# Layer 0's eight later modulation pieces in two bf16 passes, their low halves made by GpSimd, and the pieces spread over the whole input projection

## The reference, cut to what matters

```python
for layer in range(DEPTH):
    m_l = jnp.split(silu_c @ ada_w[layer] + ada_b[layer], 6, axis=-1)      # ada_w[layer]: 1024 x 6144
    m_c = jnp.split(silu_cc @ ada_w[layer] + ada_b[layer], 6, axis=-1)
    h_l = rmsnorm(x, norm_mix_g[layer]) * (1 + m_l[1]) + m_l[0]
    h_c = rmsnorm(ctx, norm_mix_g[layer]) * (1 + m_c[1]) + m_c[0]
    p_l, p_c = h_l @ w_in[layer], h_c @ w_in[layer]                        # w_in[layer]: 1024 x 3840
    ...
    x = x + m_l[2] * (mixed @ w_out[layer])
    h2 = rmsnorm(x, norm_ffn_g[layer]) * (1 + m_l[4]) + m_l[3]
    x = x + m_l[5] * channel_mixer(h2)
```

## Time and profile before

| | us |
|---|---|
| median of 3 runs | 1772.24 (1771.97 to 1772.33) |
| profiled execution, its own time | 1774.29 |
| its span, first to last instruction | 1772.4 |
| TensorE busy | 1704.0 (96%) |
| TensorE weight loads busy | 1084.0 (61%) |
| VectorE busy | 1224.6 (69%) |
| ScalarE busy | 377.2 (21%) |
| GpSimd busy | 236.2 (13%) |
| mean granted TensorE clock | 0.997 of 2.4 GHz |

### The profile page before, as it was taken

How to read it: one execution, slowest core, us unless ns; L and a number is a source line. 1 busy time by engine, 2 the same in 40 slices (tenths; PEclk the granted TensorE clock), 3 DMA queues, 4 the chain that set the end, 5 groups by cost and what they waited for, 6 DMA issues and landing times.

```text
span 1772.4 us, 34791 instructions
## 1 busy us (share of the span) xinstructions
PE 1704.0 (96%) x15369; PEld 1084.0 (61%) x15369; DVE 1224.6 (69%) x1286; ACT 377.2 (21%) x695; POOL 236.2 (13%) x108
## 2 busy tenths in 40 slices
PE   6999999899999999999999888999999999999999
PEld 2334557674544444445465555968787787869695
DVE  1443476975444344115576877999999999999998
ACT  1101254453422222112125342010100000001100
POOL 0035100020656430000460010000000000000000
PEclk9999999999999999999999999999999999999999
DMA  9932201014656425231230126999999999999994
GB/s 375 329 143 72 95 1 48 1 49 152 229 193 235 181 104 190 71 95 48 96 119 1 48 106 259 407 410 419 412 419 413 418 407 419 414 415 414 411 416 189
DMA packets 98846, 408.77 MB, mean 231 GB/s; under 512 B 14009, under 2 KB 20857, under 8 KB 84369
## 3 DMA queue, kind: packets, MB, share of 16 engines
q1 hardware_dynamic: 96504, 405.54, 58.3%
q10 hardware_dynamic: 2200, 1.08, 0.2%
HBM read 405.55 MB, written 1.05 MB: 229 GB/s over the span
## 4 chain that ended last, share of the span: by engine, by line
PE 76%; DVE 8%; PEld 5%; issue 4%; DMA 3%; ACT 2%; PEldq 0%; ACTq 0%; SPq 0%; POOL 0%; DVEq 0%; POOLq 0%
PE PS L1669 12%; PE PS L803 10%; PE PS L2044 9%; PE PS L1627 6%; PE PS L2018 5%; PE PS L2020 5%; PE PS L2021 5%; PE PS L807 5%; PE PS L1533 2%; PE PS L485 2%; DMA ARENA<-in_moe_w 2%; PE PS L1395 2%; DVE ARENA L2140 2%; PEld PS L2044 2%; DVE ARENA L1008 1%
## 5 line engine op out<-in xcount | busy, mean ns | idle before, releaser
L2140 DVE TENSOR_TENSOR ARENA<-ARENA 128x2816 bf16<-128x2816 f32 (+2 forms) x184 | 567.0, 3121 | 23.7 <-DMA ARENA<-in_moe_w 22.6
L2018 PE MATMUL PS<-ARENA 128*128 128x96 bf16 x2816 | 379.1, 209 | 4.9 <-issue 1.9
L2020 PE MATMUL PS<-ARENA 128*128 128x96 bf16 x2816 | 378.9, 209 | 1.7 <-issue 1.5
L2021 PE MATMUL PS<-ARENA 128*128 128x96 bf16 x2816 | 378.8, 206 | 1.3 <-issue 1.0
L2020 PEld LDWEIGHTS PS<-ARENA 128*128 128x128 bf16 x2816 | 354.8, 126 | 9.6 <-issue 9.5
L2018 PEld LDWEIGHTS PS<-ARENA 128*128 128x128 bf16 x2816 | 346.3, 123 | 11.6 <-issue 9.5
L2021 PEld LDWEIGHTS PS<-ARENA 128*128 128x128 bf16 x2816 | 298.6, 106 | 2.1 <-issue 2.1
L803 PE MATMUL PS<-ARENA 128*128 128x512 bf16 (+1 forms) x1104 | 227.9, 356 | 0.0
L2044 PE MATMUL PS<-ARENA 128*96 128x512 bf16 x960 | 216.1, 384 | 0.2 <-DVE ARENA L2140 0.2
L1669 PE MATMUL PS<-ARENA 128*128 128x512 bf16 x984 | 215.8, 379 | 0.0
L2044 PEld LDWEIGHTS PS<-ARENA 128*96 128x96 bf16 x960 | 116.2, 122 | 93.1 <-issue 0.3
(11 more groups left out here) (252 smaller groups left out, 1820.2 us busy)
## 6 DMA issues: line engine op xcount, KB each, us to landing
ARENA<-in_moe_w SPq DMA_DIRECT2D x128, 1408.0 KB, 13.3
ARENA<-in_moe_w SPq DMA_DIRECT2D x48, 1536.0 KB, 16.0
ARENA<-in_ada_w SPq DMA_DIRECT2D x24, 2048.0 KB, 10.2
ARENA<-in_ffn_w SPq DMA_DIRECT2D x15, 2048.0 KB, 7.9
ARENA<-in_w_in SPq DMA_DIRECT2D x11, 2048.0 KB, 8.1
ARENA<-in_moe_w SPq DMA_DIRECT2D x16, 1024.0 KB, 15.8
ARENA<-in_w_in SPq DMA_DIRECT2D x6, 1024.0 KB, 8.7
ARENA<-in_w_out SPq DMA_DIRECT2D x8, 512.0 KB, 4.3
```

The costliest lines, as they stand in the source:

```text
L2018: pe.matmul(out, hi[:, h][:, f], HEH[:, k, :], start=k == 0 and b % 4 == 0, stop=False, skip_group_check=True)
L2020: pe.matmul(out, hi[:, h][:, f], HEL[:, k, :], start=False, stop=False, skip_group_check=True)
L2021: mm = pe.matmul(out, lo[:, h][:, f], HEH[:, k, :], start=False, stop=k == KC - 1, skip_group_check=True)
L2140: dve.tensor_tensor(WLO[q % NSLOT][:, 0:n], RAW[q % NSLOT][:, 0:n], WHI[q % NSLOT][:, 0:n], ALU.subtract).then_inc(S("m_lo"), 1)
```

## The change

Layer 0's pieces 4 to 11 are treated like layer 1's: `pool_ada_halve` makes their low halves, and `pe_ada_mm` multiplies them in two bf16 passes with `SCP`. GpSimd halves pieces 4 to 9 right behind its second norm operation, piece 10 behind the inverse roots of q and k, and piece 11 between the rotations of the two latent tiles. The pieces and the two spreads get other places on TensorE, and the load of piece 11 goes to another place in SBUF (E2) and further back in SP's list.

```diff
                 if L == 0:
-                    for j in {0: (4,), 1: (5, 6, 7), 2: (8, 9), 3: (10, 11)}.get(g, ()):
-                        ada_item(0, j, ("E2", "E1")[j % 2])
+                    for j in {0: (4,), 1: (5, 6, 7), 2: (8, 9), 3: (10,), 4: (11,)}.get(g, ()):
+                        ada_item(0, j, "E1" if j in (5, 7, 9) else "E2")
...
-            if L == 0:
+            if L == 0 and j < 4:
                 parts_of, c = [ada_view(raw_full(pe, ("ada", L, j)))], SC
             else:
                 pe.wait_ge(S("filled"), 5)
-                pe.wait_ge(S("pool_halved"), KC // 2 + 2 * j + 2)
+                pe.wait_ge(S("pool_halved"), 16 + KC // 2 + 2 * j + 2 if L else 2 * (j - 4) + 2)
...
         for j in range(4, 12):
-            ADA_IN_PROJ.setdefault(((2, 3, 4, 5, 8, 9, 10, 11)[j - 4], 0), []).append(("mm", j))
-        for i, first in ((1, 6), (2, 16)):
+            ADA_IN_PROJ.setdefault(((2, 0), (3, 0), (5, 0), (6, 0), (9, 0), (10, 0), (16, 0), (19, 6))[j - 4], []).append(("mm", j))
+        for i, places in ((1, ((7, 0), (7, 2), (7, 4), (7, 6), (8, 1))), (2, ((20, 4), (21, 1), (21, 6), (22, 3), (23, 0)))):
             for step in range(5):
-                ADA_IN_PROJ.setdefault((first + (step > 1), (0, 4, 0, 3, 6)[step]), []).append(("spread", i, step))
+                ADA_IN_PROJ.setdefault(places[step], []).append(("spread", i, step))
...
             for n in range(2 * NT, 5 * NT):
-                if L == 0 and n == 3 * NT:
-                    act_ada_row(act, 0, 2)
                 act_proj_one(act, L, n)
+            if L == 0:
+                act_ada_row(act, 0, 2)
...
-                if L == 0 and n == 6:
-                    for step in range(3):
-                        dve_ada_cp(dve, 0, 1, step)
                 if L == 0 and n == 7:
-                    for step in range(3, 5):
+                    for step in range(4):
                         dve_ada_cp(dve, 0, 1, step)
                 dve_proj_one(dve, L, n)
+                if L == 0 and n == 7:
+                    dve_ada_cp(dve, 0, 1, 4)
...
-            if L == 0:
-                for step in range(5):
-                    dve_ada_cp(dve, 0, 2, step)
-                dve_ada_gain(dve, 0, 4)
             dve_proj_halve(dve, L, "av")
             if L > 0:
                 dve_gates(dve, L, 1)
             for n in range(5 * NT, 6 * NT):
+                if L == 0:
+                    for step in ((0,), (1, 2), (3,), (4,))[n - 5 * NT]:
+                        dve_ada_cp(dve, 0, 2, step)
                 dve_proj_one(dve, L, n)
+            if L == 0:
+                dve_ada_gain(dve, 0, 4)
...
             pool.tensor_tensor(STAT[:, 2, 64:88], STAT[:, 1, 64:88], NEGH[:, 0:24], ALU.pow).then_inc(S(n + "rstd"), 1)
+            if L == 0:
+                pool_ada_halve(pool, 0, 10)
             pool.wait_ge(S(n + "gained"), since(L, n + "gained") + 4)
             for x in LAT_TILES:
+                if L == 0 and x == LAT_TILES[1]:
+                    pool_ada_halve(pool, 0, 11)
...
                 pool_norm_half(pool, 2 * L, 1)
+                if L == 0:
+                    for j in range(4, 10):
+                        pool_ada_halve(pool, 0, j)
                 pool_qk(pool, L)
```

More of the change, by code:

```diff
@@ L452, in ada_halves, with pool_ada_halve @@
             return v[:, :, :, 1], v[:, :, :, 0]
-        def pool_ada_halve(pool, j):
-            raw = raw_full(pool, ("ada", 1, j))
+        def pool_ada_halve(pool, L, j):
+            raw = raw_full(pool, ("ada", L, j))
             hi, lo = ada_halves(raw)
@@ L774, in pe_proj_ready @@
                 if k % 2 == 0:
-                    pe.wait_ge(S("pool_halved"), (KC // 2 + 24) * L + k // 2 + 1)
+                    pe.wait_ge(S("pool_halved"), 16 + (KC // 2 + 24) * L + k // 2 + 1)
                 return
@@ L2370, in _ @@
                     for j in range(12):
-                        pool_ada_halve(pool, j)
+                        pool_ada_halve(pool, 1, j)
                 else:
```

## The result

| | before | changed |
|---|---|---|
| median of 8 runs each, us | 1772.38 (1771.97 to 1774.48) | 1779.24 (1776.74 to 1783.72) |
| ratio of the times | 1 | 1.0037, 95% interval 1.0025 to 1.0048 |
| profiled execution, us (span) | 1774.29 (1772.4) | 1776.84 (1775.0) |
| start of the transposes behind unit 23, us | 199.59 | 204.08 |

The changed kernel is slower by 0.37%, which is 6.6 us; the two medians are 6.9 us apart. The forecast was +2.8 us and 1775.0, its range ended at 1778.5. Its profiled execution was one of its two quickest, only 2.6 us over that of before, so it is best read for places and not for the total.

What follows compares the result with a forecast made beforehand. TensorE, busy 96% of the span, was taken to bound the kernel. Terms -0.9 up to T7, 0 to unit 16, +1.6 low clock and +2.1 behind it gave +2.8 on 1772.24: 1775.0 us, range over cases 1769.0 to 1778.5.

Steps and rivals of the forecast that it cites:

- The two signs: Prediction wrong if unit 16 starts less than 50 us after T7, or piece 5 before 65 or after 67 us.
- T7: The end of projection unit 7 on TensorE, at 109.67 us before the change, where piece 8 started.
- Step 1: Pieces 4 and 5: scalings go first, and piece 5, halved by GpSimd after landing, starts at 65.8, not 60.16; +5.6 us.
- rival (a): At 45.2 us GpSimd's halving gets in before the scalings and alternates with VectorE: +5.3 us; 0.28 together with unheld single-input operations.
- The floor at 65.8: Piece 5 lands at 58.25; 7.2 us of halving plus one or two VectorE instructions in between give 65.8.
- if single-input VectorE operations are not held: TensorE reaches unit 3 by 62 or so, stands 3 to 4 us, gets low clock: total +4.4; 0.28 together with rival (a).
- Steps 2 to 5: Pieces 5 to 7 -2.5; first spread -4.1; T7 to unit 16 0, low clock +1.6; pieces 10 and 11 +2.1 us.
- (b): At unit 16 piece 10's halving runs beside VectorE's nine operations without delaying them, no TensorE wait: -3.1 us, 1769.1; chance 0.10.
- (c): All pieces come in time: -6.6 us for pieces, -3.0 for the wait and clock at 92.68, 1762.6 us; chance 0.02.

Runs made afterwards that it cites:

- scalings first: The change with one wait more: GpSimd starts piece 4 only when VectorE has scaled the latent tokens; 1777.23 us, ratio to before 1.0019.
- 10 and 11 in f32: The change with pieces 10 and 11 left in float32 and not halved, places kept; 1774.63 us, ratio to before 1.0004.
- 4 and 5 in f32: The change with pieces 4 and 5 left in float32 and not halved, places kept; 1771.88 us, ratio to before 0.9982.
- moves alone: The change with no layer 0 piece halved, only the new places and spreads; 1771.86 us, ratio to before 0.9983.
- only 6 to 9 halved: The change with pieces 4, 5, 10 and 11 in float32; 1769.28 us, ratio to before 0.9983; once more 1767.37 us, ratio 0.9967.
- before, first group: The unchanged kernel, run beside the first group of experiments on the same chip; median 1774.26 us.
- before, second group: The unchanged kernel, run beside the second group of experiments on the same chip; median 1774.95 us.
- the change again: The changed kernel measured again without an edit; 1779.63 us, ratio to before 1.0037.
- the kernel with filler matmuls: The change plus useless matmuls, 32 before the turning of the latent tokens and 14 before unit 16; 1798.84 us, ratio to before 1.0130.

## Why the prediction was wrong

**Where each kernel is at the end of the projection.** The stages behind should only shift, so the landmark is the cleanest measure of the sum:

| kernel | transposes start | against before |
|---|---|---|
| before | 199.59 | |
| the change, two profiles | 204.08, 205.39 | +4.5, +5.8 |
| scalings first | 201.75 | +2.2 |
| 10 and 11 in f32 | 202.71 | +3.1 |
| 4 and 5 in f32 | 197.42 | -2.2 |
| moves alone | 196.35 | -3.2 |
| only 6 to 9 halved, two profiles | 192.94, 193.22 | -6.65, -6.4 |

The two signs that it named for being wrong come out one each way: piece 5 came after 67 us (68.72), unit 16 not less than 50 us after T7 (50.66).

**Step 1 failed** ("+5.6 us, a floor: the landing does not depend on anything that the change moves"). The chosen order, scalings first, did not happen; what happened was rival (a), at 0.28, in its first form: GpSimd in first, two operations alternating, 8.09 us where I had worked out 8.6. In each of the four profiles of kernels that halve piece 4 without the extra wait, GpSimd's halving starts 0.06 or 0.07 us ahead of the scaling, so this was no coin toss. Both start on the same power operation's end, at 44.9 to 45.3; the halving stands on the power's own engine, the scaling waits for a signal from another one. The row I had taken against the rival, VectorE's start 0.03 us behind that end, fits this: what stands on the same engine needed no such 0.03 us. The floor at 65.8 was worked out rightly (piece 5 was ready at 65.89) but it wasn't what bound: TensorE came at 68.7, and even in "scalings first" it came to piece 5 without a wait, late by its own low clock. "Scalings first" shows the price of the choice, 2.3 us against the change's first profile.

That the scalings are held at all rested on a case I had left open ("if single-input VectorE operations are not held"). They are: the Trainium skill (SBUF — State Buffer, Who interferes with whom) says that whoever issues first gets the shared pair for the whole instruction, and counts the two-port forms of single-input operations in; the trace agrees, with 8.09 for 1.42 us.

**The low clock was mis-sized, twice.** The prediction gave each wait the 3.2 us at half clock of the earlier trace rows, 1.6 us lost. Behind the 8.13 us wait it was 6.0 us, 3.0 lost. Behind the waits of about 3.5 us at unit 16 it was 3.1 us in one profile and 5.8 in the other, 1.5 and 2.9 lost, and in "scalings first" it was 6.8 us behind the wait of 3.60 us before piece 4. Rival (a) with 3.0 in place of 1.6 would be +6.7 and not +5.3. That this is near the +6.6 of the runs confirms nothing: the landmark of the first profile has +4.5, since TensorE's turning came 6.4 us late and not 7.2, and the steps behind it gave 1.2 us more than they were counted for.

**Steps 2 to 5 held**, but for the low clock at unit 16 in the second profile. From piece 5 to T7 it was 42.55 us where before it was 49.51: -6.96, predicted -2.5 - 4.1 = -6.6. From T7 to unit 16 it was 50.66 us (predicted 51.4), with a wait of 3.44 (predicted 4.3). VectorE's nine operations took 15.1 us (predicted about 15.5). From unit 16 to the transposes, 42.15 us for 38.53 before: +3.6, predicted 1.6 + 2.1. Piece 11 was in time, so were 7 and 9. "10 and 11 in f32" confirms that piece 10's halving alone makes the wait at unit 16. Rivals (b) and (c) did not happen.

**From +4.5 at the landmark to +6.6 in the runs.** Each run lists its span and its mean granted clock; span x (1 - clock) is the time that low clock stands for in it. The clock is listed to 0.001, which is 1.8 us, so a single run says little and a mean more. Of the 8 runs before beside the change only times are on record, so its row has to be compared with the other groups. The means:

| kernel (runs) | span | of it by low clock | the rest |
|---|---|---|---|
| before, first group (32) | 1772.4 | 4.1 | 1768.3 |
| before, second group (23) | 1773.0 | 4.4 | 1768.6 |
| the change (8) | 1777.8 | 9.6 | 1768.2 |
| the change again (11 of 12) | 1778.0 | 10.2 | 1767.8 |
| scalings first (12) | 1775.8 | 8.4 | 1767.4 |
| 10 and 11 in f32 (12) | 1773.5 | 7.1 | 1766.4 |
| 4 and 5 in f32 (12) | 1770.1 | 5.0 | 1765.1 |
| moves alone (11) | 1770.0 | 2.9 | 1767.1 |
| only 6 to 9, two groups (8 of 9, and 5) | 1767.0, 1766.3 | 3.5, 2.8 | 1763.5, 1763.5 |

(Left out are the single runs of 1800.42 and 1790.33, with clocks of 0.981 and 0.983.) The rest is the same before and after the change, within 0.8 us, and what is left over, 5.5 to 5.8 us, is the low clock's column. About 2.0 us of it lie in the wait from 49.0 to 53.1 (4.1 us at 0.50) and are in truth the wait's. So the shorter pieces and the spreads' places paid for all but some 2 us of the waiting, and the low clock cost TensorE some 3.5 us more than before. The prediction's own sum had nothing for this in all, 1.6 off at the first spread and 1.6 on at unit 16, and rival (a) had 1.6. The profiled execution of the change, at 1775.0 x 0.004 = 7.1, has 2.5 us less of it than the mean of its runs, which is why its span understates the change: the kernel before lost 1.7 us in its own profile to a low-clock stretch near 1080 us that the change's first profile lacks. In the second profile the excess lies in longer stretches at the places of the change and in stretches near 24, 925 and 1086 us. The kernel before has such a one at 24 us and one at 1078 us too, behind the same wait of 2.08 us, so these are not the change's doing as such; whether it makes them likelier was not tested and stays open.

## What to carry to other kernels

Work given to an idle helper engine is not free while it shares something with the engine that feeds the bound one: before it is queued, look whom it can get ahead of, and where the feeder has a short operation that the bound engine waits for, put that first by an explicit wait (2.3 us here). Of the two engines that waited for the same end, the one on which it ended started first in every profile here. Halve only the pieces that have slack: four of the eight gave their full 3.3 us, the other four turned a gain of 6.5 us at the landmark into a loss of 4.5 to 5.8. And price a new wait of TensorE as its length plus half of the low-clock stretch behind it, as a range and not a number: behind waits of 3.4 us and more the stretch was 3.1 to 6.8 us here, and behind shorter ones (1.38, 1.62, 2.08 us) it came in some cases and not in others.

## What the runs showed of the hardware that I had not expected

- Single-input f32 VectorE operations between SBUF tiles are held by a GpSimd tensor_tensor, a small one for as long as a large one: 4.08 us for a 128x1024 scaling (0.71 alone), 3.45 us for 128x8 (0.17 alone).
- Back to back VectorE operations don't always alternate with GpSimd's. At 45 us and at 142 us they did; at 890 us GpSimd's short operation waited 8.89 us for a train of them. What decides this was not tested.
- The same wait at the same place (3.44 and 3.56 us) was followed by 3.1 us at half clock once and by 5.8 us another time; one of 2.08 us, near 1080 us, by some 3.4 us in the kernel before and in the change's second profile, and by none in its first.
- In the kernel with filler matmuls the clock stayed at 0.50 for 57.4 us of nearly unbroken work (56.2 us busy), where every other low clock seen in the projection ended within 7 us of TensorE's return to work. Its cause is open.
